# Outputs of a state recurrence with blocks as rows and a turn on TensorE, and rotated q and k stored by residue class

## The reference, cut to what matters

```
# even mixer: two halves, concatenated and multiplied by even_w_out
y_a = _ssd_mixer(zxbcdt, ...)      # 8 heads of 64; ends with y * silu(z), then an RMS norm over groups of 256 channels
y_b = _s5_mixer(u, ...)            # 32 groups of 16 channels with 64 complex states each
#   h[t] = abar * h[t-1] + B u[t];   y = Re-part(C h) + d_skip * u
#   gate = gelu(y) @ w_glu + b_glu;  result y * sigmoid(gate)

# hybrid mixer: three attention groups with (window, dilation) (128, 1), (512, 4), (2048, 16)
q, k = apply_rotary(q), apply_rotary(k)      # x1 cos - x2 sin, x2 cos + x1 sin over half heads of 32
o, lse = dilated_window_attention(q, k, v, window, dilation)     # 8 heads of 64; by residue class of t mod dilation
```

## Time and profile before

| | |
|---|---|
| median of 3 runs | 2978.79 us |
| range of the runs | 2972.84 to 2979.21 us |
| time of the profiled execution | 2975.73 us |
| its span | 2973.9 us |
| mean granted TensorE clock, share of full speed | 0.971 |
| TensorE matmul busy | 2810.5 us, 95% of the span |
| VectorE busy | 1459.1 us, 49% |
| ScalarE busy | 949.5 us, 32% |

### The profile page before, as it was taken

How to read it: one execution, slowest core, us unless ns; L and a number is a source line. 1 busy time by engine, 2 the same in 40 slices (tenths; PEclk the granted TensorE clock), 3 DMA queues, 4 the chain that set the end, 5 groups by cost and what they waited for, 6 DMA issues and landing times. The chain is left out here.

```text
span 2973.9 us, 34050 instructions
## 1 busy us (share of the span) xinstructions
PE 2810.5 (95%) x12640; PEld 2245.9 (76%) x12640; DVE 1459.1 (49%) x1894; ACT 949.5 (32%) x1287; POOL 202.2 (7%) x209
## 2 busy tenths in 40 slices
PE   6999999969999999999988999999999999699997
PEld 5788777547888878888766788887777677488885
DVE  5566347655444344443475544423887335433323
ACT  4432223233333233322234333222224442333212
POOL 3000114101000000000210000000000000000000
PEclk9999999779999999999999999999999999799998
DMA  3344325223333222332311233333441133133321
GB/s 120 113 124 135 126 97 161 62 85 93 99 99 104 94 83 94 99 106 92 110 50 43 92 99 96 114 104 110 135 124 44 43 99 99 47 95 99 106 96 38
DMA packets 82457, 284.69 MB, mean 96 GB/s; under 512 B 14753, under 2 KB 15393, under 8 KB 81473
## 3 DMA queue, kind: packets, MB, share of 16 engines
q1 hardware_dynamic: 71424, 250.54, 26.7%
q0 software_dynamic: 6336, 26.70, 2.8%
q10 hardware_dynamic: 4608, 6.30, 0.9%
HBM read 262.26 MB, written 14.94 MB: 93 GB/s over the span
## 5 line engine op out<-in xcount | busy, mean ns | idle before, releaser
L177 DVE TENSOR_TENSOR wl<-raw,wh 128x1024 fp32r<-128x1024 f32 (+2 forms) x440 | 574.2, 1306 | 1062.7 <-ACT wh L171 1051.8
L223 PE MATMUL PS<-Hh,wl 128*128 128x512 f32 x2232 | 879.7, 394 | 44.2 <-DVE wl L177 20.5
L224 PE MATMUL PS<-Hh,wh 128*128 128x512 f32 x2232 | 872.5, 391 | 0.0
L225 PE MATMUL PS<-Hl,wh 128*128 128x512 f32 x2232 | 872.4, 391 | 0.0
L171 ACT ACTIVATE wh<-raw 128x1024 fp32r<-128x1024 f32 (+2 forms) x440 | 480.1, 1091 | 1145.3 <-PE PS L225 975.5
L223 PEld LDWEIGHTS PS<-Hh,wl 128*128 128x128 f32 x2232 | 421.3, 189 | 148.8 <-issue 51.7
L225 PEld LDWEIGHTS PS<-Hl,wh 128*128 128x128 f32 x2232 | 421.1, 189 | 88.8
L224 PEld LDWEIGHTS PS<-Hh,wh 128*128 128x128 f32 x2232 | 421.5, 189 | 87.8 <-issue 1.5
L225 PE MATMUL PS<-ffn_gl,wh 128*128 128x512 f32 x880 | 350.5, 398 | 0.0
L223 PE MATMUL PS<-ffn_gh,wl 128*128 128x512 f32 x880 | 346.1, 393 | 2.8 <-DVE wl L177 2.8
L224 PE MATMUL PS<-ffn_gh,wh 128*128 128x512 f32 x880 | 348.2, 396 | 0.0
(11 more groups left out here) (409 smaller groups left out, 2599.1 us busy)
## 6 DMA issues: line engine op xcount, KB each, us to landing
raw<-in_gu SPq DMA_DIRECT2D x220, 512.0 KB, 3.6
raw<-in_dn SPq DMA_DIRECT2D x80, 704.0 KB, 4.1
raw<-in_hin SPq DMA_DIRECT2D x44, 512.0 KB, 4.3
raw<-in_oin SPq DMA_DIRECT2D x16, 512.0 KB, 3.7
raw<-in_hin_gate SPq DMA_DIRECT2D x16, 512.0 KB, 3.6
X<-QKV ACTq DMA_DIRECT2D x96, 64.0 KB, 3.2
kept_x<-X POOLq DMA_DIRECT2D x16, 256.0 KB, 3.6
raw<-in_eout SPq DMA_DIRECT2D x8, 512.0 KB, 3.7
```

What stands on the lines that cost most here:

```text
L177: self.nc.vector.tensor_sub(self.wl[j % SPLIT][:, 0:kw], self.raw[j][:, 0:kw], self.wh[j % SPLIT][:, 0:kw].bitcast(F32)).then_inc(self.lo_ ...
L223: self.nc.tensor.matmul(out, wl, xh[:, u.k0 + k, :], start=first, stop=False)
L224: self.nc.tensor.matmul(out, wh, xh[:, u.k0 + k, :], start=False, stop=False)
L225: done = self.nc.tensor.matmul(out, wh, xl[:, u.k0 + k, :], start=False, stop=last)
```

## The change

Outputs are computed with the operands exchanged: the inputs `U8[:, g, :]` and the states `SB` are the weights (128x64), `TOE` and `OUT` are streamed with 128 columns, and two groups g and g+4 write partitions 0 to 63 and 64 to 127 of bank 3. ScalarE evicts them, permuted, to `YB(q)`, and 16 matmuls with the identity (64x64 blocks, `turn_outputs`) turn them into bank 3 again, now with channels as rows. `add_input(q)` reads PSUM. The DRAM tensor `s5_y` with its 32 stores and 4 loads is gone. All four quarters are added and given their gelu within `states_and_heads`; three of the four squares move there too; in `finish_halves` the sums of squares stand ahead of the `w_glu` product. The order on TensorE becomes outputs(q-1), heads(q-1), turn_outputs(q-1), swap of states. `TOE` is now kept by group (its table `KT` is copied unpermuted).

In the hybrid input, the four DMAs of unit n are issued at the head of `read(n + 1)`, ahead of its wait for TensorE, and for n of 8 and more the sum of `rotate` writes `QKV` by class, so that `window_attend` reads contiguous 128 columns.

```
@@ S5Tables.act
-                a.activation(self.KT.rearrange("p (i g) -> p g i", g=S5G),
-                             self.co.PS[:, 7, :].rearrange("p (g i) -> p g i", i=16), ACT.Copy).then_inc(self.k_evicted, 1)
+                a.activation(self.KT, self.co.PS[:, 7, :], ACT.Copy).then_inc(self.k_evicted, 1)
@@ states_and_heads
+        SQ = YL[:].rearrange("p c l b -> p c (l b)")
-        Y8 = lambda q: DRIVE[:, 8 * q:8 * q + 4, :].rearrange("p g n -> p (g n)") if q < 3 else XC[:, 7, :]
+        YB = lambda q: DRIVE[:, 8 * q:8 * q + 4, :].rearrange("p g n -> p (g n)")
@@ sync
-            for q in range(4):
-                sp.wait_ge(evicted, q + 1)
-                for l in range(BL):
-                    to = d["s5_y"].rearrange("(g i) l b -> l i g b", i=16)[l, :, 8 * q:8 * q + 8, :]
-                    sp.dma_start(to, Y8(q)[16 * l:16 * l + 16, :].rearrange("p (g b) -> p g b", b=NB)).then_inc(stored, 16)
-                if q < 3:
-                    sp.wait_ge(stored, 16 * BL * (q + 1))
-                    sp.dma_start(YL[:, q], d["s5_y"][q * P:(q + 1) * P]).then_inc(restored, 16)
@@ tensor, outputs(q)
                 if q >= 1:
-                    pe.wait_ge(evicted, q)
-                for g in range(8 * q, 8 * q + 8):
-                    out = co.PS[:, 3, NB * (g % 8):NB * (g % 8) + NB]
-                    mm(out, TOE[:, :, g::S5G].rearrange("p l i -> p (l i)"), U8[:, g, :], start=True, stop=False)
-                    m = mm(out, OUT[:, g, :], SB[:, q % 2, g % 8, 0:NB], start=False, stop=True)
+                    pe.wait_ge(added, q)
+                for j in range(4):
+                    out = lambda s: co.PS[NB * s:NB * s + NB, 3, j * P:(j + 1) * P]
+                    for s in range(2):
+                        g = 8 * q + 4 * s + j
+                        mm(out(s), U8[:, g, :], TOE[:, :, 16 * g:16 * g + 16], start=True, stop=False)
+                    for s in range(2):
+                        g = 8 * q + 4 * s + j
+                        m = mm(out(s), SB[:, q % 2, g % 8, 0:NB], OUT[:, g, :], start=False, stop=True)
                 m.then_inc(out_done, 1)
+
+            def turn_outputs(q):
+                pe.wait_ge(evicted, q + 1)
+                for l in range(BL):
+                    for s in range(2):
+                        p = NB * s
+                        m = mm(co.PS[p:p + NB, 3, NB * l:NB * l + NB], YB(q)[p:p + NB, NB * l:NB * l + NB],
+                               co.ident[p:p + NB, p:p + NB], start=True, stop=True)
+                m.then_inc(out_turned, 1)
@@ tensor, the loop over q and its end
                 if q >= 1:
+                    outputs(q - 1)
                     heads(q - 1)
-                    outputs(q - 1)
+                    turn_outputs(q - 1)
                 swap_states(q)
             outputs(3)
             heads(3)
+            turn_outputs(3)
@@ scalar
-                nc.scalar.activation(Y8(q), co.PS[:, 3, :], ACT.Copy).then_inc(evicted, 1)
+                nc.scalar.activation(YB(q).rearrange("p (l j i) -> p j l i", l=BL, i=16),
+                                     co.PS[:, 3, :].rearrange("p (j l i) -> p j l i", l=BL, i=16),
+                                     ACT.Copy).then_inc(evicted, 1)
+
+            def square(c):
+                act.wait_ge(gated, c + 1)
+                act.wait_ge(out_done, c + 1)
+                nc.scalar.activation(SQ[:, c, :], XC[:, c, :], ACT.Square).then_inc(squared, 1)
                 power(2 * q + 1)
+                if q >= 2:
+                    square(q - 2)
             evict(3)
-            for c in range(3):
+            square(2)
+            for c in range(4):
                 act.wait_ge(added, c + 1)
@@ vector
             def add_input(q):
-                dve.wait_ge(restored, 16 * (q + 1))
+                dve.wait_ge(out_turned, q + 1)
                 dve.wait_ge(gated, q + 1)
-                through(co, v, U, YL, Z, q, cols).then_inc(added, 1)
+                k = cols["s5_d"] + q
+                v.scalar_tensor_tensor(Z[:, q, :].rearrange("p (b l) -> p l b", l=BL), U[:, q], co.cols[:, k:k + 1],
+                                       co.PS[:, 3, :].rearrange("p (l b) -> p l b", b=NB), ALU.mult,
+                                       ALU.add).then_inc(added, 1)
                 if q >= 1:
                     skip(q - 1)
-                if q >= 2:
-                    add_input(q - 2)
-            add_input(2)
+                    add_input(q - 1)
             skip(3)
+            add_input(3)
@@ finish_halves, sync and tensor
-            sp.wait_ge(stored, 16 * BL * 4)
-            sp.dma_start(YL[:, 3], co.dram["s5_y"][3 * P:4 * P]).then_inc(brought, 16)
             co.load(sp, st)
-            sp.wait_ge(brought, 16)
...
-            co.multiply(pe, st, bank_free, chunk_ready=g_parted, between=sums)
+            pe.wait_ge(squared, 1)
+            for c in range(4):
+                m = nc.tensor.matmul(co.PS[:, 4 + c // 2, :], co.ones[:], SQ[:, c, :], start=c % 2 == 0, stop=c % 2 == 1)
+            m.then_inc(summed, 1)
+            co.multiply(pe, st, bank_free, chunk_ready=g_parted)
@@ finish_halves, scalar (vector: part_g(0..3) with nothing between)
-            for c in range(3):
-                round_g(c)
-            for c in range(4):
-                nc.scalar.activation(SQ[:, c, :], Y[:, c, :], ACT.Square).then_inc(squared, 1)
-            act.wait_ge(skipped, 1)
-            nc.scalar.activation(T[:, 3, :], YB[:, 3, :], ACT.Gelu_apprx_tanh).then_inc(gelued, 1)
-            act.wait_ge(gelued, 1)
-            round_g(3)
+            nc.scalar.activation(SQ[:, 3, :], Y[:, 3, :], ACT.Square).then_inc(squared, 1)
+            for c in range(4):
+                round_g(c)
@@ window_attend, scores
-                        m = mm(co.PS[:, 2 * (k % 2) + s, (1 + g) * P:(2 + g) * P], QKV[p:p + HD, 8 * g + c, r::4],
-                               QKV[p:p + HD, 8 * g + 4 + c, r::4], start=True, stop=True)
+                        m = mm(co.PS[:, 2 * (k % 2) + s, (1 + g) * P:(2 + g) * P], QKV[p:p + HD, 8 * g + c, r * P:(r + 1) * P],
+                               QKV[p:p + HD, 8 * g + 4 + c, r * P:(r + 1) * P], start=True, stop=True)
@@ hybrid_input, scalar
+            def swap(n):
+                c = n % RAW
+                if n >= RAW:
+                    act.wait_ge(done, n - RAW + 1)
+                for q in range(4):
+                    p, o = 32 * q, 32 * (q ^ 1)
+                    act.dma_start(B[p:p + 32, c], QKV[o:o + 32, n:n + 1, :]).then_inc(swapped[c], 16)
...
                     if n == 0:
                         act.wait_ge(gated, RAW)
+                    else:
+                        swap(n - 1)
                     co.wait_units(act, st, i, c)
                     nc.scalar.activation(one(QKV, n), one(co.PS, c), ACT.Copy).then_inc(taken, 1)
                     act.wait_ge(taken, n + 1)
                     act.sem_inc(bank_free, 1)
-                    if i > first_qk:
-                        act.wait_ge(done, RAW * (i - first_qk - 1) + c + 1)
-                    for q in range(4):
-                        p, o = 32 * q, 32 * (q ^ 1)
-                        act.dma_start(B[p:p + 32, c], QKV[o:o + 32, n:n + 1, :]).then_inc(swapped[c], 16)
+                elif i == first_v and c == 0:
+                    swap(RAW * (first_v - first_qk) - 1)
@@ hybrid_input, vector, rotate(n)
-                nc.vector.tensor_add(one(QKV, n), A[c % 2], B[:, c]).then_inc(done, 1)
+                to = one(QKV, n) if n < 8 else QKV[:, n, :].rearrange("p (r q) -> p q r", r=4)
+                by = (lambda t: t) if n < 8 else (lambda t: t.rearrange("p o (q r) -> p (o q) r", r=4))
+                nc.vector.tensor_add(to, by(A[c % 2]), by(B[:, c])).then_inc(done, 1)
```

More of the change, by code:

```diff
@@ L1567, in _, with finish_halves @@
                     skip(q - 1)
-                if q >= 2:
-                    add_input(q - 2)
-            add_input(2)
+                    add_input(q - 1)
             skip(3)
-def through(co, v, U, YL, YB, c, cols):
-    k = cols["s5_d"] + c
-    return v.scalar_tensor_tensor(YB[:, c, :].rearrange("p (b l) -> p l b", l=BL), U[:, c], co.cols[:, k:k + 1],
-                                  YL[:, c], ALU.mult, ALU.add)
+            add_input(3)
 @stage
-def finish_halves(co, st, Y, YB, U, YL, T, SQ, M, cols, stored):
+def finish_halves(co, st, Y, YB, T, SQ, M, cols):
     nc = co.nc
@@ L1591, in finish_halves @@
             u.x = G
[L1592 to L1596 removed]
+        (squared, summed, scaled, rooted, inverted, g_rounded, g_parted, normed, rounded, parted, bank_free, gates, gated,
+         y_rounded) = (
+            co.sem(f"fin_{s}") for s in ("squared", "summed", "scaled", "rooted", "inverted", "g_rounded", "g_parted",
+                                         "normed", "rounded", "parted", "bank_free", "gates", "gated", "y_rounded"))
         restored = co.soft_sem("fin_restored")
@@ L1613, in _ @@
         def _(pe):
-            def sums(n):
```

(14 more changed lines are left out.)

21 lines of the change are left out of this document (7 added, 14 removed).

## The result

The changed kernel takes 2948.66 us (median of 4, 2947.81 to 2950.76) where the kernel before takes 2977.53 on the same chip: ratio 0.9907, 95% interval 0.9889 to 0.9924. The span of the profiled execution falls from 2973.9 to 2947.7 us.

The account below looks back on a forecast made before the run. TensorE, busy for 95% of the span, was taken as the bound, with waits in three stretches. -0.4 - 7.4 - 5.5 = -13.3 us gives 2962.4 from the profiled execution, 2965.5 from the median; predicted 2965, range 2954 to 2974.

Parts of the forecast that it names:

- part one: Recurrence and the stage behind it: new outputs and their way back, forecast -0.4 us, bounds +4 and -7.
- The bound of -3.8: Recurrence loop: most that outputs and turns of two quarters could save, what VectorE's idle time allows.
- The bound of +1.6: Recurrence loop: worst case for the same two quarters, both at half clock with the turn at its upper bound.
- The added wait: Recurrence, last quarter: outputs(3) reuses bank 3, waits for quarter 2's add, and starts at 605.9 rather than 603.16.
- The cover for rounding and splitting under the sums: Stage behind the recurrence: sums of 3.6 us hide some 2.8 us of rounding and splitting gelus.
- Part two: Hybrid input: later DMA issues end TensorE's stalls, 8.0 us, less 0.6 for the last rotation: -7.4 us.
- Part three: Window attention: packed reads save 0.63 us per pair of steps; -5.5 us, bounds -3 and -9.
- The clock stays up: Rival, chance 0.13: denser outputs and less idling keep TensorE's clock up, -7 in part one, -20 in all, 2959.
- The state stage loses: Rival, chance 0.14: added wait and half-clock turns cost +5 us in the recurrence stage; -8 in all, 2970.5.
- the stall: Rival, chance 0.11: hybrid input keeps its stall, -2 instead of -7.4 us; -8 in all, 2970.5.
- the slow write: Rival, chance 0.04: hybrid input's sum written with a step of 128 elements takes 2.6 us, giving 2986.
- no effect: Rival, chance 0.05: each part of the change is hidden and nothing is gained, 2979.

Follow-up runs that it names:

- bank_apart: Changed kernel with outputs, eviction, turn and add of quarter 3 in bank 0, so outputs(3) needn't wait for quarter 2's add: 2944.61 us, ratio 0.9893.
- sums_late: Changed kernel with the sums of squares back between the first and second unit of the w_glu product: 2953.09 us, ratio 0.9928.
- state: Kernel before plus only the recurrence edits (everything of the diff up to finish_halves), hybrid input as before: 2964.23 us, ratio 0.9961.
- swap: Kernel before plus only the four DMAs of a unit moved to the head of the next read: 2965.71 us, ratio 0.9967.
- packed_load: Kernel before with the L1428 weights loaded from 128 consecutive TOE elements, not with a stride of 32 (wrong values): ratio 0.9971.
- exchange: Kernel before with the outputs' operands exchanged and KT copied unpermuted, old place and way over DRAM kept (results land in wrong places): ratio 0.9944.

## Why the prediction was wrong

The direction was right; the size wasn't. Forecast were -0.4, -7.4 and -5.5 us, and the stretches have -12.2, -9.2 and -2.5: the error is in part one, and those of the other two nearly cancel.

- **The step that failed** is "A quarter of the loop then costs 3.65 instead of 5.31 (-1.7) at the full clock, and 7.3 instead of 6.83 (+0.5) at half ... one at each level makes -1.2, bounds -3.8 ... and +1.6". It prices outputs and turn as if the clock of the work around them were given, and puts that work at nothing. Measured, the states of quarter 2 are ready 8.7 us earlier (30.8 against 39.6), and those of quarter 3, 7.6 earlier. Of the 8.7, outputs and turn of two quarters make 2.2 (4.54 instead of 5.91, 4.46 instead of 5.30), near the 1.2 of the sum. The rest is other work at the full clock instead of half: drives, spreads and swap of drives 4.5, heads 3.4, swaps of states 0.8, of which new waits take 2.1 back. In the kernel before the clock falls inside the outputs of quarter 0 and stays at half for 17 us; with packed loads, or exchanged operands, it doesn't. The bound of -3.8 came from VectorE's idle time of 3.77 us at 587.46. The one a quarter earlier, which I hadn't looked at, is longer, as the row below shows. The first two quarters are 20.1 and 19.5 us long, the third 14.2; their difference in length was the row that would have shown 11 us to be won. (The bound of +1.6 is also added up wrongly: by its own terms, 3.9 and 3.9 against 6.83, twice, it is +1.9.)

```profile
567.96 0.69 DVE L1526 TENSOR_TENSOR DTV<-PS,X 128x512 f32<-128x512 f32 x1 [5.32 <-PE PS L1417]
```

- **The added wait** was placed right: `outputs(3)` was to start 4.7 us after its states (605.9 against 602.41 - 1.2); it started 4.99 after. It is a loss of 5.1 us that `bank_apart` takes back.
- **Behind it** the trace has outputs 3.44, heads 2.65, turn 1.08, handovers and gelu 3.4, sums 5.4 (with the scaling's handover), 16.0 us in all, where I had 3.9, 4.54, 3.4, 3.6 and 5.0, 20.4. The turn was mis-sized most: 0.034 us a record at the full clock instead of 0.053, and it ran at the full clock all four times, where I had half; that the clock came back during `heads(3)` was not in the sum. The scaling thus came at 21.0 us after the states, where before it was 24.3.
- **Sums first** hold: -3.5 us in the stretch by `sums_late`, -4.4 from the states of quarter 3 to the scaling. The cover for rounding and splitting under the sums held too: VectorE's split (2.50 us at 612.15) ended before the scaling.
- **Part two** was forecast at -7.4, and the trace has -9.2: all stalls go (8.1), and the last rotation, for which I had subtracted 0.6, waited 1.02 us for its DMA; with the taps behind it TensorE waits 0.79 us for `wl` in the token units, less than before, and the stage gained 1.1 there instead. The four issues take 2.44 us beside the split, as forecast. The sum is 1.10 us, as taken. By the Trainium skill, SBUF — State Buffer (the note on cachelines), each access on a new 16-byte line pays a penalty, so that every step from four fp32 elements up should cost the same. The trace agrees: 1.07 us with a step of 4, 1.10 with 128.
- **Part three** was forecast at -5.5. The changed kernel has -2.5 in the stretch. The saving per scores block is 0.58 instead of 0.63. By the 11 steps that agree it is 3.5, 0.32 a step, nearly the 0.31 that I had taken; the four ahead of them gain nothing in this trace, and 0.8 are given back behind the last scores.
- **The rivals.** *The clock stays up* was nearest, at a chance of 0.13, and even it was sized at -7 for part one, and its reason, less idling, isn't what the trace shows: the outputs themselves run at half the clock all four times, and what gained is the work around them. The argument against it, that the added wait makes idling longer, is true: 1.36, 1.66 and 6.25 us before the outputs of quarters 1 to 3, each time with the lower clock behind it. The first costs nothing, since VectorE sets the pace there (14.4 us from states to states); behind the second it waits 0.92 us for the heads; the last lies on the path. *The state stage loses* is refuted by `state` (-11.6), the stall by `swap`, the slow write by 1.10 us, no effect by the ratio. Of a drain at a change of tiling mode (the Trainium skill, TensorEngine Tiling (Array Packing), Tiling Modes) the trace still shows nothing: the turn starts at 576.88, and the heads ahead of it are busy from 574.61 for 2.34 us, with no idle time between.

Not settled: what brings the clock down. The five traces with strided loads in the old place (the kernel before and the four that don't touch the recurrence) all lose it some 3 us into the outputs of quarter 0 and for 17 us; `packed_load` and `exchange` don't. But the same strided blocks of quarters 1 and 2 keep the full clock, and `packed_load` loses it elsewhere, twice, for some 3.4 us. So the loads are not the whole cause, and what the chip measures isn't shown. Nor do the runs show why the last window steps lose the full clock with packed reads, after a wait that was no longer than before.

## What to carry to other kernels

When one iteration of a loop is longer than another with the same work, look at the granted clock of each block before pricing anything: here most of the gain lay in blocks whose code the edit didn't touch, and which were priced at nothing. Price weights loaded with a stride at both levels of the clock: packed loads gained 0.21 us in 0.66 at the full one and nothing at half. Before calling a small difference an effect, see whether it lies in a part that the edit touches. A buffer that is reused in the last iteration, where nothing hides the wait, deserves a bank of its own if one is free.

## What the runs showed of the hardware

- A float32 weight load of 128x128 with a stride of 32 elements takes 0.31 us by the median where the packed one takes 0.19 (`packed_load`). At half the clock a block of 32 records takes no longer with the strided loads (6.83 us, mostly at half, against 7.02). Streaming the same slice shows no cost at half the clock (96.5 us for the stretch both ways).
- Products with 64-column weights, side by side in the two halves of the array, are 0.055 us a record apart at the full clock and 0.107 at half; turns of 64x64 with the identity 0.034 at the full clock.
- The granted clock can fall from 1.00 to half within a run of matmuls without idle time (563.2 in the kernel before; 569.7 and 583.5 in `packed_load`), while outputs ran at the full clock behind 2.00 us of idle time (`bank_apart`, 597.48) and at half behind 1.36 (571.23, after).
- The four swap DMAs of a unit land in 2.0 us by the median when issued beside the split, where they took 3.2 right after the copy.
